# Six instead of seven heads of tile 0 summed on VectorE, forgetting scores issued in couples, and a fifth late query head: one Trainium2 core

## The reference, cut to what matters

```python
h   = x + concat(forgetting_attention(8 heads of 64), differential_attention(4 heads, two maps each)) @ w_out
hn  = rmsnorm(h, norm2_g)
# channel mixer, for each token and each of 8 heads:
q = (hn @ peer_w_q).reshape(128, 8, 2, 128)
sc = einsum('thpd,hpkd->thpk', q, sub_keys)       # two lists of 128 scores
s1, i1 = top_k(sc[:, :, 0], 16); s2, i2 = top_k(sc[:, :, 1], 16)
top_s, pos = top_k(s1[..., :, None] + s2[..., None, :], 16)   # 16 of 16384 experts
g   = softmax(top_s)
hid = gelu(einsum('thkd,td->thk', u_tab[eidx], hn)) * g
h   = h + einsum('thk,thkd->td', hid, v_tab[eidx])
out = rmsnorm(h, final_g)
```

## Time and profile before

| what | value |
|---|---|
| time, median of 3 runs | 1541.17 us (1539.67 to 1543.49) |
| the profiled execution's own time | 1541.62 us |
| its span in the trace | 1539.8 us |
| TensorE, VectorE, ScalarE, GpSimd busy | 82%, 70%, 30%, 49% |
| read from HBM | 593.54 MB, 387 GB/s over the span |

### The profile page before, as it was taken

How to read it: one execution, slowest core, us unless ns; L and a number is a source line. 1 busy time by engine, 2 the same in 40 slices (tenths; PEclk the granted TensorE clock), 3 DMA queues, 4 the chain that set the end, 5 groups by cost and what they waited for, 6 DMA issues and landing times.

```text
span 1539.8 us, 13062 instructions
## 1 busy us (share of the span) xinstructions
PE 1269.3 (82%) x3727; PEld 658.2 (43%) x3727; DVE 1077.6 (70%) x2520; ACT 459.8 (30%) x1200; POOL 751.5 (49%) x637
## 2 busy tenths in 40 slices
PE   9999999988888488999787777677886787777778
PEld 7766655665545234444333333233332233332333
DVE  3247699999988867566666676666666766666654
ACT  3432355466343022222222222221222222222212
POOL 0016477675667443454544554445444554444440
PEclk9999999999989699999899999989999999999998
DMA  9669799997999999999999999999999999999995
GB/s 382 250 250 413 275 330 351 370 376 268 340 371 392 391 421 416 421 421 421 421 422 422 421 422 421 421 422 421 422 421 421 422 422 421 422 420 422 421 421 208
DMA packets 99741, 596.50 MB, mean 387 GB/s; under 512 B 11480, under 2 KB 11480, under 8 KB 42328
## 3 DMA queue, kind: packets, MB, share of 16 engines
q0 software_dynamic: 89856, 536.91, 86.0%
q1 hardware_dynamic: 9816, 58.77, 9.6%
HBM read 593.54 MB, written 2.10 MB: 387 GB/s over the span
## 4 chain that ended last, share of the span: by engine, by line
DMA 42%; PE 15%; DVE 6%; POOL 3%; issue 2%; ACT 2%; DVEq 0%; POOLq 0%
PE acc L994 13%; DMA map_mem<-in_peer_uv_dram,eidx 10%; DMA w_ring<-in_peer_uv_dram,eidx 9%; DMA v_all<-in_peer_uv_dram,eidx 7%; DMA act_mem<-in_peer_uv_dram,eidx 6%; DMA v_ring<-in_peer_uv_dram,eidx 3%; DMA mix_mem<-in_peer_uv_dram,eidx 3%; DMA u_ring<-in_peer_uv_dram,eidx 3%; DMA v_ring<-in_peer_v_dram,eidx 2%; PE mm L786 1%; ACT diag L1228 1%; DVE map_mem L1549 1%; DVE w_ring L1549 1%; PE sc L786 1%; POOL v_ring L692 1%
## 5 line engine op out<-in xcount | busy, mean ns | idle before, releaser
L1220 ACT ACTIVATE gel<-hid 128x4 f32<-128x4 f32 x126 | 25.8, 205 | 722.2 <-DVE hid L1549 712.5
L685 POOL DMA_INDIRECT u_ring<-in_peer_u_dram,eidx x112 | 136.8, 1221 | 172.9 <-DVE eidx L1529 99.5
L994 PE MATMUL acc<-v_all,diag 128*128 128x512 f32 x256 | 129.2, 651 | 61.1 <-ACT diag L1228 60.6
L692 POOL DMA_INDIRECT v_ring<-in_peer_v_dram,eidx x112 | 133.4, 1192 | 66.4 <-DVE h L1577 38.0
L1577 DVE SCALAR_TENSOR_TENSOR h<-v_ring,coef,h 128x1024 f32<-128x1024 f32 x112 | 143.9, 1284 | 14.3 <-DMA v_ring<-in_peer_v_dram,eidx 11.3
L994 PE MATMUL acc<-map_mem,diag 128*128 128x512 f32 x248 | 123.3, 644 | 32.0 <-ACT diag L1228 32.0
L994 PE MATMUL acc<-v_ring,diag 128*128 128x512 f32 x248 | 120.1, 629 | 32.3 <-ACT diag L1228 28.7
L1541 DVE CUSTOM_DVE_ANT_0 u_ring<-u_ring,hn 128x1024 f32<-128x1024 f32 x112 | 136.6, 1220 | 14.2 <-DMA u_ring<-in_peer_u_dram,eidx 14.0
L994 PE MATMUL acc<-u_ring,diag 128*128 128x512 f32 x248 | 119.1, 626 | 27.4 <-ACT diag L1228 25.8
L1228 ACT ACTIVATE diag<-ident,coef 128x128 f32<-128x128 f32 x392 | 126.3, 390 | 39.1 <-DVE coef L1567 30.8
L711 POOL DMA_INDIRECT v_all<-in_peer_uv_dram,eidx x64 | 76.1, 1189 | 92.3 <-PE acc L994 81.7
(11 more groups left out here) (281 smaller groups left out, 2331.9 us busy)
## 6 DMA issues: line engine op xcount, KB each, us to landing
w_ring<-in_slabs_dram SPq DMA_DIRECT2D x29, 1024.0 KB, 8.4
v_ring<-in_slabs_dram SPq DMA_DIRECT2D x6, 1024.0 KB, 11.2
u_ring<-in_slabs_dram SPq DMA_DIRECT2D x6, 1024.0 KB, 10.9
map_mem<-in_slabs_dram SPq DMA_DIRECT2D x6, 1024.0 KB, 7.9
h<-in_x_dram SPq DMA_DIRECT2D x4, 512.0 KB, 12.5
u_ring<-in_peer_u_dram,eidx POOLq DMA_INDIRECT x112, 6.9
v_ring<-in_peer_v_dram,eidx POOLq DMA_INDIRECT x112, 7.1
v_all<-in_x_cols_dram SPq DMA_DIRECT2D x3, 512.0 KB, 7.4
```

The source lines that it names most:

```text
L685: nc.gpsimd.indirect_dma_start(out=u_ring[:, c % U_RING, :], out_offset=None, in_=peer_u[0], in_offset=bass.IndirectOffsetOnAxis(ap=eidx[n ...
L692: nc.gpsimd.indirect_dma_start(out=v_ring[:, c % V_RING, :], out_offset=None, in_=peer_v[0], in_offset=bass.IndirectOffsetOnAxis(ap=eidx[n ...
L994: last = nc.tensor.matmul(acc[half][:, :], diag[:, c % COLS, :], v_row(n, c)[:, half * BANK:(half + 1) * BANK], start=first, stop=(n % PH ...
L1220: nc.scalar.activation(gel[:, par, g0:g0 + COLS], hid[:, par, g0:g0 + COLS], ACT.Gelu).then_inc(gelu_done, 1)
```

## The change

`HOST_HEADS` goes from 7 to 6, so one more head of tile 0 is done with rows of 8 KB: the row phase has 26 heads, and the later pieces are spread over 24 slots instead of 28. `LATE_HEADS` goes from 4 to 5: head 3 of tiles 1 to 3 gets its queries and keys in the row phase. The half of `store` that holds tile 0's key scores is no longer free when the first rows of 8 KB are gathered, since head 7's search has still to read it. It goes from the free places to the end of the ring of ten, with a wait on the first half of that search. Forgetting scores of heads 2i and 2i + 1 are issued together at the even step: both q times k, then both gate terms.

```diff
-HOST_HEADS = 7
+HOST_HEADS = 6
-LATE_HEADS = 4
+LATE_HEADS = 5
...
-        row_mem += [store[:, 0:PH * 2 * K1], mix_mem[:, :]]
+        row_mem += [mix_mem[:, :]]
         FREE_ROWS = len(row_mem)
         row_mem += [m for flat in (ur_flat, vr_flat) for m in halves_of(flat)]
+        row_mem += [store[:, 0:PH * 2 * K1]]
         RING = len(row_mem)
...
+                elif place == RING - 1:
+                    pool.wait_ge(topk_step, TK * (PH - 1) + TK_FIRST)
...
+            def pair_scores(g, step):
+                t, first = at_step(g, 0, step)
+                nk, j = P * (t + 1), GROUPS[g].index(t)
+                if first == 0:
+                    pe.wait_ge(selq_ready, 2 * (t + 1))
+                both = [(HD * (m % 2), m // 2, map_no[(t, m)]) for m in (first, first + 1)]
+                for lo, ch, k in both:
+                    if k >= len(sc_b):
+                        pe.wait_ge(sc_drained, k + 1 - len(sc_b))
+                    nc.tensor.matmul(sc_b[k % len(sc_b)][:, 0:nk], qT[lo:lo + HD, ch, j * P:(j + 1) * P], kv_t[lo:lo + HD, ch, 0:nk],
+                                     start=True, stop=False)
+                for lo, ch, k in both:
+                    nc.tensor.matmul(sc_b[k % len(sc_b)][:, 0:nk], selq[lo:lo + 40, ch, t % 2, :], caug[lo:lo + 40, 0:nk],
+                                     start=False, stop=True).then_inc(sc_full, 1)
...
             def scores(g, half, step):
-                if at_step(g, half, step):
+                if half == 0:
+                    if step % 2 == 0 and at_step(g, half, step):
+                        pair_scores(g, step)
+                elif at_step(g, half, step):
```

More of the change, by code:

```diff
@@ L602, in build @@
         TK_IDX = 21
+        TK_FIRST = 10
         PARTS = 9
@@ L912, in attend @@
                 values(g, half, step)
+            def pair_scores(g, step):
[12 more added lines that the diff above has]
+                                     start=False, stop=True).then_inc(sc_full, 1)
             def scores(g, half, step):
-                if at_step(g, half, step):
+                if half == 0:
+                    if step % 2 == 0 and at_step(g, half, step):
+                        pair_scores(g, step)
+                elif at_step(g, half, step):
                     t, it = at_step(g, half, step)
                     nk, j = P * (t + 1), GROUPS[g].index(t)
-                    if it == 0:
-                        pe.wait_ge(selq_ready, 2 * (t + 1))
                     for m in maps_of(it):
@@ L923, in scores @@
                             pe.wait_ge(sc_drained, k + 1 - len(sc_b))
[L924 to L934, removed]
+                        lo, ch = HD * ((m - FH) % 2), KC // 2 + (m - FH) // 2
+                        nc.tensor.matmul(sc_b[k % len(sc_b)][:, 0:nk], qT[lo:lo + HD, ch, j * P:(j + 1) * P], kv_t[lo:lo + HD, ch, 0:nk],
+                                         start=True, stop=True).then_inc(sc_full, 1)
             def turned_map(g, half, step):
```

## The result

The changed kernel takes 1549.12 us (median of 5 runs, 1548.33 to 1552.87), the kernel before in the same comparison 1542.39. The ratio is 1.005, 95% interval 1.0033 to 1.0067: slower by half a per cent. The forecast was 1539 with a range of 1533 to 1547. The profiled execution took 1548.33 us, its span is 1546.5 against 1539.8: 6.7 us more. Of the 10.1 us between forecast and result, 1.2 lie in the kernel before itself, whose median was 1541.17 when the forecast was made.

A forecast was written before the change was run, and what follows sets the result against it. It took TensorE up to the forget piece, VectorE through the hosted stage, then gathers at 421 GB/s as bounds. Terms -41.0 + 42.4 - 1.4 + 0 - 2.0 + 0 = -2.0 us; forecast 1539 us, range 1533 to 1547.

The forecast's parts named there:

- The bound: Hosted stage, 178 to 485 us: VectorE, working 292 of 307 us, sets the time behind the forget piece.
- First scores of tile 1: Behind the value projections: a new VectorE wait of 2.7 us, later score waits of 1.7 and 0.9 go; taken as 0.
- sign of being wrong: Mark set in advance against the forecast: VectorE idle over 8 us for scores.
- VectorE's side: Behind the forget piece: fewer dots, additions and coefficient products and one search fewer, 41.0 us less.
- The late chain: Queries and gelu late in the hosted stage: the 4.8 us gelu wait falls to about 0 to 1; 2.0 us less.
- The DMA's side: Row phase: sixteen more rows (39.9 us) and the fifth late head's slab (2.5 us) at 421 GB/s, 42.4 us more.
- Row places: Change to the row phase: one row fewer in flight, taken as 0, bounds 0 and 2.5 us more.
- Paired scores: Tile 0, ahead of the forget piece: two forgetting heads together cost TensorE what one did, 1.4 us less.
- The clock in the late chain: Rival: late-chain queries 0 to 2 all at 1.2 GHz, a gelu wait of 13 us, 1549 us; chance 0.13.
- The pairing gives nothing: Rival: adjacent heads overlap already or bank waits take the saving back, 1541 us; chance 0.10.
- The rate of 358 GB/s: Rival: transfers from HBM are held to the skill page's lower rate, 1547 us; chance 0.03.

The follow-up runs named there:

- e9: Kernel before with VectorE relieved, one hosted addition in four adding only half of the row: 1539.8 us, ratio 0.9985.
- e8: Changed kernel with VectorE relieved, one hosted addition in four adding only half of the row: 1545.4 us, ratio 1.0026.
- g3: Changed kernel with one hosted addition in four over half the row and eight projections adding up 5 of 8 chunks: 1539.6 us, ratio 0.9994.
- e1: Changed kernel without the couples, every forgetting score issued by itself: 1557.4 us, ratio 1.0101.
- g1: Changed kernel with TensorE relieved, eight hosted-stage projections adding up 5 of 8 chunks: 1545.6 us, ratio 1.0029.
- f4: Kernel before with the row place in the store half moved to the end of the ring of ten: 1542.6 us, ratio 1.0010.
- g2: Kernel before with TensorE relieved, eight hosted-stage projections adding up 5 of 8 chunks: 1541.8 us, ratio 0.9999.
- e2: Kernel before with the couples alone, seven hosted heads and four late heads: 1545.8 us, ratio 1.0027.

## Why the prediction was wrong, step by step

- **The bound.** The failed step is "Behind the forget piece VectorE is the bound", read from 292 busy of 307 us. The same row has TensorE at 279 of 307 us and the DMA share at 0.92, neither of which the prediction weighed. e9 shows the price: 13.2 us of VectorE's work are worth 2.1. What the runs show in its place is that VectorE, TensorE and, near the end of the stage, the gathers hold each other up: work taken from VectorE comes back as waits for the others (e8, e9), and both reliefs together give more than either (g3).
- **First scores of tile 1.** This term, taken at 0 with bounds of 2.6 less and 4.0 more, is where that step broke in the sum. The first wait was sized well (2.7 forecast, 2.5 measured). The later ones did not "go, since TensorE gets through the couples sooner": they grew, and all score waits by 10.9 us. e1 shows that the couples lessen them, g1 that TensorE's load makes 6.8 us of them. That they grew because the list now stands in 24 slots instead of 28 is argued, not shown. The prediction's own sign of being wrong, VectorE idle over 8 us for scores, came with 14.6. The output projection's wait of 3.5 us had no term.
- **VectorE's side.** The count was right: 41.0 us of work, 42.2 measured. Only 36.6 shortened the stage.
- **The late chain.** -2.0 forecast, 1.0 more measured: the first gelu wait was 1.3, near the 0 to 1 worked out, but two more came behind it (3.1 and 1.4). The waits for gathers fell by 10.4; the sum had only some 2.5 of that, in the row places. Without this fall the miss would have been larger, so the forecast came as near as it did partly by luck.
- **The DMA's side.** Right: 421 GB/s held, and 42.4 plus the row place's upper bound of 2.5 is the 44.9 measured. **Row places** were taken at 0; f4 gives 2.7 in the trace of one execution and 0.7 in the median, so that the 2.5 are theirs is not shown.
- **Paired scores** ahead of z_f: 1.5 for 1.4, partly by luck. With the same work of TensorE up to there z_f came between 171.7 and 174.2 us in four traces (the changed kernel, e8, g1, g3) and between 172.5 and 173.8 in four others (the kernel before, e9, f4, g2), so one trace of each can't settle 1.5.
- **Rivals.** The clock in the late chain has the right time, 1549 us, by a wrong mechanism: the gelu waits are 5.8 us, the longest 3.1, not 13. "The pairing gives nothing" is refuted with six heads by e1; with seven the couples gained nothing and cost 0.27% (e2). The rate of 358 GB/s is refuted by 421 over 980 us. The Trainium skill (HBM Reference, Specifications) has about 425 GB/s for a core that streams alone, and the row agrees with that.

## What to carry to other kernels

An engine that is 95% busy need not be the bound: where a second one is 91% busy, the DMA has a share of 0.92 and each waits for the others' results, work taken from one turns into waits. Make one engine lighter in a trial run and see what comes back before counting its time in full. Test the parts of a change in more than one order: here the hosted head cost 0.1% behind the other two parts and 1.2% without the late head. Where a table of shares spreads pieces over slots, taking one piece out moves all others; with six late heads, moving the forget piece and what follows it was worth some 13 us here.

## What the runs showed of the hardware

A TensorE wait of 2 to 3 us ahead of a projection was paid twice. Behind the wait of 2.19 us above the projection took 6.7 us; behind two other waits of the changed kernel:

```profile
234.29 0.52 PE L963 MATMUL tr<-ident,map_mem 128*128 128x128 f32 x3 [2.96 <-ACT map_mem L1201]
235.65 6.67 PE L790 MATMUL acc<-act_mem,w_ring 128*128 128x384 f32 x16
...
276.40 1.94 PE L985 MATMUL o<-v_all,map_mem 128*128 128x64 f32 x8 [2.99 <-DVE mix_mem L1466]
278.14 7.60 PE L790 MATMUL mm<-act_mem,w_ring 128*128 128x384 f32 x16
```

With no such wait ahead it took 5.4. The granted clock was 0.57 for the 5 us around the first wait's end, a mean near the lower of its two levels (1.2 and 2.4 GHz, or 0.5 and 1.0). Where TensorE's work was made lighter its clock was lower (0.91 instead of 0.96 in g2 from 174 to 300 us), and all in all TensorE was busy for only 5.6 us less there (287.5 to 281.9 from 174 to 490 us). That its longer pauses lowered the clock is argued, not shown: no run changes the pauses alone.
